# Modulation chunks by channels: each column group makes 128 channels over all of k, and a transpose takes the place of the summing products

## The reference, cut to what matters

```python
def _layer(x, c, ...):
    mod = (jax.nn.silu(c) @ w_ada + b_ada).reshape(bsz, N_MOD, 1, D_MODEL)
    sh1, sc1, gt1, sh2, sc2, gt2 = (mod[:, n] for n in range(6))
    hn = _rmsnorm(x, g_norm1) * (1.0 + sc1) + sh1
    proj = hn @ w_in                                  # 2048 -> 5120
    q, k, v, xl, gl = jnp.split(proj, [...], axis=-1)
    attn = attn_fn(_rmsnorm(q, g_q), _rmsnorm(k, g_k), v, b_sb)   # 8 heads of 128
    lru = rglru(causal_dwconv(xl)) * jax.nn.gelu(gl)
    x = x + gt1 * (jnp.concatenate([attn, lru], axis=-1) @ w_out) # 2048 -> 2048
    hn2 = _rmsnorm(x, g_norm2) * (1.0 + sc2) + sh2
    u = causal_dwconv(hn2 @ w_up)                     # 2048 -> 12288
    ug, uv = jnp.split(u, 2, axis=-1)
    x = x + gt2 * ((jax.nn.gelu(ug) * uv) @ w_down)   # 6144 -> 2048
```

## Time and profile before

| | |
|---|---|
| median of 3 runs | 2901.7 us (2900.48 to 2905.5) |
| span of the profiled execution | 2902.6 us |
| TensorE busy | 2828.4 us (97%), 24051 instructions |
| weight loads of TensorE | 2695.1 us (93%) |
| DVE, ACT, POOL busy | 61%, 41%, 10% |
| DMA | 444.51 MB, mean 153 GB/s |
| mean granted clock of TensorE | 0.992 of full |

### The profile page before, as it was taken

The page is one execution under the profiler, slowest core; times in us unless marked ns, Lnnn a source line. Parts: engine busy times, 40 slices in busy tenths (PEclk is TensorE's granted clock), DMA queues, the critical chain, the costliest instruction groups (busy, mean ns, idle before and its releaser), DMA issues.

```text
span 2902.6 us, 60828 instructions
## 1 busy us (share of the span) xinstructions
PE 2828.4 (97%) x24051; PEld 2695.1 (93%) x24051; DVE 1769.2 (61%) x2752; ACT 1189.4 (41%) x1458; POOL 280.8 (10%) x532
## 2 busy tenths in 40 slices
PE   5999999999999999799999999999999999999999
PEld 3689999878888999699999999999999999999999
DVE  3433433544534433888888888888888755555553
ACT  3244444545444322644444444444444422222222
POOL 0000000112221000011111111111111000000000
PEclk9999999999999999899999999999999999999999
DMA  9985555377667655633333333333333633333323
GB/s 360 318 264 168 159 162 167 109 230 233 217 222 235 197 158 169 201 115 100 112 105 113 99 117 105 109 100 117 111 102 106 210 109 108 106 107 110 106 82 110
DMA packets 608980, 444.51 MB, mean 153 GB/s; under 512 B 14569, under 2 KB 556127, under 8 KB 607469
## 3 DMA queue, kind: packets, MB, share of 16 engines
q1 hardware_dynamic: 585602, 363.97, 41.2%
q0 software_dynamic: 22176, 77.86, 8.2%
q10 hardware_dynamic: 1044, 0.43, 0.1%
HBM read 408.14 MB, written 34.06 MB: 152 GB/s over the span
## 4 chain that ended last, share of the span: by engine, by line
PE 92%; DVE 3%; DMA 2%; ACT 2%; issue 1%; SPq 0%; DVEq 0%; ACTq 0%; POOLq 0%
PE ps L808 45%; PE ps L1265 36%; PE ps L824 2%; PE ps L1101 1%; PE ps L1067 1%; PE ps L1052 1%; PE ps L904 1%; PE ps L1056 1%; PE ps L932 1%; DMA wide_act<-in_w_ada_dram 1%; PE ps L848 1%; PE ps L966 1%; DMA page<-in_cache_k_dram 0%; PE ps L944 0%; DMA raw<-in_w_in_dram 0%
## 5 line engine op out<-in xcount | busy, mean ns | idle before, releaser
L1265 PE MATMUL ps<-ops,w_hi 128*128 128x288 f32 x4608 | 921.0, 296 | 0.5 <-DVE w_lo L2334 0.5
L1265 PEld LDWEIGHTS ps<-ops,w_hi 128*128 128x128 f32 x4608 | 741.7, 189 | 0.9 <-DVE w_lo L2334 0.9
L1265 PE MATMUL ps<-ops,w_lo 128*128 128x288 f32 x2304 | 679.4, 295 | 0.0
L1929 DVE TENSOR_TENSOR w_lo<-raw,w_hi 128x1024 fp32r<-128x1024 f32 x240 | 293.2, 1225 | 575.4 <-ACT w_hi L1377 575.3
L808 PE MATMUL ps<-gs,w_hi 128*128 128x288 f32 x3072 | 607.1, 294 | 0.0
L808 PE MATMUL ps<-act_hi,w_hi 128*128 128x288 f32 x1792 | 544.7, 304 | 8.4 <-DVE w_lo L1929 3.1
L808 PE MATMUL ps<-act_lo,w_hi 128*128 128x288 f32 x1792 | 528.9, 295 | 0.0
L808 PE MATMUL ps<-act_hi,w_lo 128*128 128x288 f32 x1792 | 528.1, 295 | 0.0
L1377 ACT ACTIVATE w_hi<-raw 128x1024 fp32r<-128x1024 f32 x240 | 253.4, 1058 | 657.3 <-PE ps L808 639.8
L808 PEld LDWEIGHTS ps<-gs,w_hi 128*128 128x128 f32 x3072 | 490.3, 188 | 0.0
L808 PE MATMUL ps<-gs,w_lo 128*128 128x288 f32 x1536 | 451.3, 294 | 0.0
(11 more groups left out here) (377 smaller groups left out, 3130.7 us busy)
## 6 DMA issues: line engine op xcount, KB each, us to landing
raw<-in_w_up_dram SPq DMA_DIRECT2D x120, 512.0 KB, 4.3
raw<-in_w_down_dram SPq DMA_DIRECT2D x128, 384.0 KB, 3.2
raw<-in_w_in_dram SPq DMA_DIRECT2D x80, 512.0 KB, 5.8
ada_q<-in_w_ada_dram SPq DMA_DIRECT2D x80, 512.0 KB, 5.4
page<-in_cache_v_dram POOLq DMA_DIRECT2D x64, 512.0 KB, 4.7
page<-in_cache_k_dram POOLq DMA_DIRECT2D x52, 512.0 KB, 4.7
ax<-in_w_up_dram SPq DMA_DIRECT2D x48, 512.0 KB, 4.9
wide_act<-in_w_ada_dram SPq DMA_DIRECT2D x22, 1024.0 KB, 12.2
```

Of the source, the lines that this page charges most:

```text
L1265: mm = pe.matmul(ps[:, bank, 0:HALF], w[slot][:, kk, :], moving(i, kk, low), start=i not in ADDED and kk == 0 and w is w_hi and not low, s ...
L1929: dve.tensor_tensor(w_lo[s][:], raw[s][:], w_hi[s][:].bitcast(F32), ALU.subtract).then_inc(lo_done, 1)
```

## The change

The 512 channels of four chunks are now made together. Group j makes the 128 channels of chunk j over all 16 k tiles, so the result is 128 partitions (4 chunks by 32) by 128 channels, with the sum over k complete. One transpose then puts the channels of all four chunks on the partitions, at a pitch of 32 columns. A load unit is as large as a chunk was (1 MB, two halves), but holds 4 k tiles by 512 channels, in pieces of 2 KB where a chunk's are of 512 bytes; four units make a quad of 512 channels. A wide product of 512 columns becomes four of 128.

The heads make one quad each, four units: two add up in one bank, two in another, and DVE adds the two. The unit behind the turn of the keys and values is gone. The output projection makes five quads, 20 units, five for each quarter of 8 blocks, behind products 0, 2, 3, 4 and 6. The far part makes three quads. `sel` goes.

```diff
-OUT_AFTER = (0, 2, 6)
+OUT_AFTER = (0, 2, 3, 4, 6)
+OUT_QUAD = {(0, 2): 0, (1, 1): 1, (2, 1): 2, (3, 0): 3, (3, 3): 4}
+OUT_TURN = {(1, 0): 0, (2, 0): 1, (3, 0): 2, (3, 1): 3}
-M_QKV, M_OUT = 32, 72
+M_QKV, M_OUT = 32, 64
+def quad_bank(n):
+    return 7 - (n // 4) % 2
...
-            def ada_chunk(ring, m, n):
+            def ada_unit(ring, n):
+                q, quad = n % 4, M_QKV // 4 + n // 4
                 for h in range(2):
                     slot = 2 * (n % 2) + h
...
                     wait(sp, sem("ada_used"), 2 * n + h - 3)
-                    sp.dma_start(ring[:, slot, :, :], wa_v[:, h * KB:(h + 1) * KB, m * P:(m + 1) * P]) \
+                    sp.dma_start(ring[:, slot].rearrange("p (a b) c -> p a (b c)", a=2),
+                                 wa_v[:, 4 * q + 2 * h:4 * q + 2 * h + 2, 512 * quad:512 * quad + 512]) \
                       .then_inc(sem(f"ada_loaded{slot}"), 16)
...
+            def unit_products(out, q, h, w, begin, end):
+                w = w.rearrange("p (a b) c -> p a (b c)", a=2)
+                for a in range(2):
+                    for j in range(4):
+                        mm = pe.matmul(out[32 * j:32 * j + CW, :], cs[:, 4 * q + 2 * h + a, :], w[:, a, j * P:(j + 1) * P],
+                                       start=begin and h == 0 and a == 0, stop=end and h == 1 and a == 1, skip_group_check=True)
+                return mm
...
-                    for kk in range(KB):
-                        j = kk % 4
-                        mm = pe.matmul(ps[32 * j:32 * j + CW, bank, R0:R0 + P], cs[:, h * KB + kk, :], ring[:, slot, kk, :],
-                                       start=False, stop=h == 1 and kk >= 4, skip_group_check=True)
-                    mm.then_inc(sem("ada_used"), 1)
+                    unit_products(out, n % 4, h, ring[:, slot], begin, end).then_inc(sem("ada_used"), 1)
...
-            def turn_mod(rows, n, bank, t, c=448):
+            def turn_mod(rows, bank, t, c):
                 pe.wait_ge(sem("rows_taken"), t + 1)
-                for j in range(n):
-                    mm = pe.matmul(ps[:, bank, c + CB * j:c + CB * (j + 1)], rows[:, j, :], sel[:], start=True, stop=True)
+                for j, row in enumerate(rows):
+                    mm = pe.transpose(ps[:, bank, c + j * P:c + (j + 1) * P], row, ident[:])
                 mm.then_inc(sem("mod_turned"), 1)
...
-                    for j in range(WK):
-                        mm = pe.matmul(ps[32 * j:32 * j + CW, bank, :], cs[:, WK * q + j, :], wide(b)[:, j, :],
-                                       start=q == 0, stop=q == 3, skip_group_check=True)
+                    for k in range(WK):
+                        for j in range(4):
+                            mm = pe.matmul(ps[32 * j:32 * j + CW, bank, 0:P], cs[:, WK * q + k, :], wide(b)[:, k, j * P:(j + 1) * P],
+                                           start=q == 0 and k == 0, stop=q == 3 and k == WK - 1, skip_group_check=True)
...
                 pe.wait_ge(sem("k_out"), 3 * i + 3)
                 turn_kv(i)
-                ada_chunk(ada_q, n + 4, 0)
...
+                    if 2 * j + 1 in OUT_AFTER:
+                        out_unit(n)
+                        n += 1
...
-                act.wait_ge(sem("q_out"), 3 * i + 3)
-                act.wait_ge(sem("k_out"), 3 * i + 3)
-                ins = act.activation(mod_rows_q[:, 4, :], ps[:, 0, R0:R0 + P], ACT.Copy)
-                ins.then_inc(sem("v_out"), 1)
...
                     take_k(i)
+                dve.wait_ge(sem("q_out"), 3 * i + 3)
+                dve.wait_ge(sem("k_out"), 3 * i + 3)
+                dve.tensor_tensor(mod_rows_q[:, 2, :], mod_rows_q[:, 0, :], mod_rows_q[:, 1, :], ALU.add).then_inc(sem("rows_taken"), 1)
                 lo(u, 9)
```

More of the change, by code:

```diff
@@ L622, in _ @@
             qkv_block(10)
-            chunk(7)
+            unit_of(6)
             qkv_block(11)
-            chunk(8)
+            unit_of(7)
             qkv_block(12)
@@ L663, in _ @@
                 out_block(b)
-            n = 5 * NH
-            ada_chunk(ada_o, M_QKV + n, n)
+            n = 4 * NH
+            ada_unit(ada_o, n)
             n += 1
@@ L815, in product, with ada_unit @@
                     mm.then_inc(blk_used, 1)
-            def ada_chunk(ring, n, bank):
+            def unit_products(out, q, h, w, begin, end):
[5 more added lines that the diff above has]
+                return mm
+            def ada_unit(ring, n, out, begin=False, end=False):
                 for h in range(2):
@@ L1202, in sum2, with out_unit @@
                     mm.then_inc(sem("sq2_used"), 1)
+            def out_unit(n):
+                ada_unit(ada_o, n, ps[:, quad_bank(n), 0:P], begin=n % 4 == 0, end=n % 4 == 3)
             def start_two(u, n):
@@ L1226, in out @@
                         product(u, 2 * j, gps[j % 2], act_hi, act_lo, last=False)
-                    if j == 0 and not first:
-                        turn_mod(mod_rows_o, 3, 4, 15 + i)
+                    if (i, j) in OUT_TURN:
+                        a = OUT_TURN[i, j]
+                        turn_mod([mod_rows_o[:, a, :]], 4, 16 + a, 0)
                     if not lead and 2 * j in OUT_AFTER:
-                        ada_chunk(ada_o, n, 2 * (j % 2))
+                        out_unit(n)
                     if 2 * j in OUT_AFTER:
@@ L1295, in up_tile @@
                         pe.wait_ge(sem("lnew_taken"), 2)
-                        turn_mod(rows_far, FAR, 4, 20, c=300)
+                        turn_mod([rows_far[:, a, :] for a in range(3)], 4, 21, 0)
                     if i == 6:
@@ L2361, in out @@
                     k, m = 2 * j, 4 * i + j
-                    n, c = sum(a < k for a in OUT_AFTER), sum(a // 2 == j for a in OUT_AFTER)
                     if i < 3 or j < 2:
```

147 lines of the change are left out of this document (65 added, 82 removed).

## The result

| | before | changed |
|---|---|---|
| median, same chip | 2903.6 us (2900.48 to 2906.03, 4 runs) | 2885.6 us (2883.2 to 2888.03, 4 runs) |
| ratio, 95% interval | | 0.9932 (0.992 to 0.9944) |
| span of the profiled execution | 2902.6 us | 2886.5 us |
| TensorE busy | 2828.4 us | 2811.2 us |
| DMA packets | 608980 | 510681 |

It is 18.0 us faster by the medians and 16.1 by the two traces, where 12.2 were forecast. The forecast counted from 2901.7, the median of three runs of the kernel before; with a fourth run it is 2903.6. That the time is nearly the 2885.4 of rival (d) is chance: the stop that (d) denied is there, and nearly half of what was gained beyond the forecast came from the heads.

What follows compares the result with a forecast made beforehand. TensorE was taken as the bound, 92% of the chain of waits. Terms -10.9 - 7.3 - 0.8 (head 8's turn) - 1.4 + 10.3 - 2.1 = -12.2 us from 2901.7 gave 2889.5 us, range 2881 to 2896.5.

Steps and rivals of the forecast that it cites:

- rival (d): Output projection: no stop because 2 KB pieces land in time, clock stays; 2885.4 us, chance 0.13.
- Heads 2 to 7: Each head loses a chunk (1.01) and 0.81 of the turn, 1.82 us, six times: -10.9 us.
- Heads 0 and 1: Earlier weight load shrinks head 1's wait (-2.6), clock spell goes, chunks and turn are saved: -7.3 us.
- The 1.75 for the clock: Head 1's scores: without the wait, no spell at 1.2 GHz, so 2.35 us instead of 4.10: -1.75.
- Rival (a): Head 1 keeps its wait because the load lands earlier only as TensorE comes earlier; 2893.9 us, chance 0.13.
- Opening: Last turn shorter (-0.6) and last wide loads sooner (-0.8), together -1.4 us; wide products unchanged.
- two shorter turns let them start 0.8 to 1.6 us sooner: Opening: the last four wide loads, waiting for products, start sooner; bounds 0 to -1.6, taken as -0.8 us.
- Output projection: Seven units +7.1, the third unit of the first quarter +3.1, clock spell +1.0, turns -0.9: +10.3 us.
- the third unit: First quarter of the output projection: TensorE waits for its late load, +3.1 us, bounds +0 to +3.9.
- The spell at 1.2 GHz (+1.0): Output projection: slow clock after TensorE idles at the third unit, more likely than not, +1.0 of at most 1.75.
- Rival (b): Ring of two units starves the output projection, stopping TensorE in each quarter: +6.3, 2895.8 us, chance 0.10.
- Begin of the FFN: The far turn of twelve chunks, 2.58 us, becomes three transposes of 0.4 together: -2.1 us.
- Rival (c): New units' column groups do not overlap, 3.6 us a unit instead of 1.01: +135, about 3024 us, chance 0.04.

Runs made afterwards that it cites:

- experiment 5: Changed kernel with the turn of heads 1 to 8 done as five fp32 products, not one transpose: 2895.17 us, period 53.68 instead of 52.78.
- experiment 6: Changed kernel with one more unit's products, without a load, in heads 1 to 7 behind the turn of keys and values: 2895.44 us, period 53.98.
- experiment 12: The kernel before, unaltered and profiled once more: one execution of 2902.13 us, span 2900.4.
- Experiment 3: Changed kernel with the opening's wide products of 512 columns again, four to a block; turns stay one transpose each: 2888.57 us.
- experiment 10: The changed kernel once more, unaltered: 2887.14 us.
- experiment 11: Changed kernel with units behind products 0, 2, 4, 5, 6 in the first quarter of the output projection alone: 2887.41 us.
- experiment 2: Changed kernel, each unit waiting for both halves of its load and running one column group after the other: 2957.79 us.
- Experiment 1: Changed kernel with units in heads and output projection loaded in pieces of 512 bytes instead of 2 KB (modulation not that of the reference): 2889.21 us.
- experiment 7: Changed kernel with units behind products 0, 2, 4, 5, 6 instead of 0, 2, 3, 4, 6 in every quarter of the output projection: 2893.0 us.
- experiment 9: Changed kernel with units paired in heads and output projection, quarters 2 to 4 with the second pair behind product 3 instead of 4: 2882.61 us.

## Why the forecast held, and where it missed

- **Heads 2 to 7**, -10.9 forecast, -12.68 measured to head 8's scores. The mechanism held: every microsecond taken from TensorE there was one of time (experiments 5 and 6 put it back and paid it in full in the period). Two prices were too small. The chunk was priced at its own row, 1.01, and is worth 1.2 with the product behind it (experiment 6); the turn was taken at 0.2 with the argument that a lone transpose pays for entering, and costs 0.11: the 0.59 of the earlier trace rows was not the price of a first transpose in this place.
- **Heads 0 and 1**, -7.3 forecast. To head 2's scores -9.27 against -9.5, so this step and the opening together came right, with two errors that cancel: the opening gave 0.2 instead of 1.4, heads 0 and 1 with head 2's turn 9.07 instead of 8.1. The late weight block came 6.1 us earlier, more than the 4.5 worked out, so nothing of the wait was left (0.5 forecast). The 1.75 for the clock was a gain against that one trace: in experiment 12 a wait of nearly the same length brought no spell, and against that trace heads 0 and 1 gained 8.1 and not 9.1. That this step came so close is in part luck. Rival (a) fell: no trace with the new order has a wait for the modulation at head 1's scores.
- **Opening**, -1.4 forecast, -0.2 measured. The failed step is "two shorter turns let them start 0.8 to 1.6 us sooner", counted as a gain at the last landing. Experiment 3 doesn't settle it. The first two of the last four loads were issued 1.6 and 2.1 us sooner (97.43 and 98.91 against 99.04 and 101.02), the last 0.7 later; but in the second trace of the kernel before those two went out at 96.55 and 98.54, with the long turns. Where the last landing is in the chain it lies anywhere from 113.4 to 117.0 us. What makes that scatter stays open, and the traces show no gain in the opening that is larger than it.
- **Output projection**, +10.3 forecast, +7.96 measured. The term that was most mis-sized is the third unit, +3.1: product 4 came 0.9 us later behind the release (1.6 in experiment 10), about what the unit alone costs, so that the new stop mostly stood in the place of the 1.7 us for which TensorE had waited for DVE. The landing was worked out from one trace in which it was late, 16.3 us behind the release; the second trace of before has 14.6, and 2 KB pieces take off 0.6 to 1.5 more (the 0.8 in the forecast is 0.9 by its own rates). The spell at 1.2 GHz (+1.0) did not come. Against that the seven other units cost 1.2 and not 1.01 each (+1.4), and the turns were 0.4 cheaper: 7*1.2 + 0.9 - (3*0.57 - 4*0.11) = 8.0. Rival (b) fell: no TensorE wait for a unit's load in quarters 2 to 4. Rival (d), no stop, fell as well: there is one, and taking it away was no gain (experiment 11), so its price of 4.1 us was wrong too.
- **Begin of the FFN**, -2.1 forecast, -2.4 measured together with the spells around it (-3.3 against experiment 10); the turn itself 2.58 to 0.33.
- **Rival (c)** fell at once, 1.01 a unit, but experiment 2 shows its mechanism real, at 2.39 us instead of 3.6.
- **The rule on pieces.** The Trainium skill (DMA: Bandwidth & Descriptors, Specifications) gives 512 bytes as the least transfer for line rate, by which 512-byte and 2 KB pieces would run alike. Experiment 1 sides against it, mildly: product 4 came 0.6 to 1.5 us later with the short pieces.

The medians differ by 18.0 and 17.5 us, the traces by 16.1 (and 14.8 between experiments 10 and 12). The traced execution of the changed kernel was the slowest of its four, 2888.03 us, which is 2.4 above their median. Two stretches scatter from trace to trace: the opening (it ends between 116.9 and 120.0 us) and the stretch from head 8's scores to the release (416.6 to 420.5 us); the period and the way from release to last row repeat within 0.1 and 0.7 us for one kernel. What makes the two stretches scatter stays open.

## To carry to other kernels

Price a small piece of work between large ones by taking it out of the sum with what stands behind it: the row of the piece shows 1.01 us, the period shows 1.20. Before a wait is charged, ask which wait it replaces; here the new one stood where TensorE had waited for DVE anyway, and removing it gave nothing. Before a landing or a spell at the slow clock is priced, read it in more than one trace: the landing behind the third unit's price and the spell behind head 1's came from one. And in a queue that is served in order, moving a use by one product moves every load behind the reload of its buffer, up to the next stage: experiment 7 lost about 5 us that way, and in experiment 9 moving a use forward took away a wait of 1.8 us, though the gain in time is within the noise.

## What the runs showed of the hardware

- Sixteen fp32 products of 32 stationary columns by 128 moved ones take 1.01 us when neighbours use different column groups, 2.39 when four in a row use the same one.
- What follows a unit takes 0.20 us longer than behind other work: a product 6.56 against 6.36, the scores 2.35 against 2.15 (behind a product). Two units back to back take 1.89. Why is not shown.
- A lone fp32 transpose of 128x128 between a product and a unit costs 0.11 us.
- The same loads in pieces of 512 bytes landed 14.7 us behind the release, in pieces of 2 KB 13.2 to 14.1 in six traces.
- A wait of 3.1 us was followed by a spell at 1.2 GHz in one execution of the kernel before (mean granted clock 0.71 over 5 us), and one of 2.6 us by none in another (1.00).
